# Three edits at the start of a two-block transformer kernel: where the first modulation is summed, how its weights are loaded, and which banks the MLPs' first chunk uses

## What is computed

```python
c_act = silu(c)
for l in range(2):
    mod = c_act @ w_ada[l] + b_ada[l]                   # 1024 x 6144 weights
    shift1, scale1, gate1, shift2, scale2, gate2 = split(mod, 6)
    hdn = rmsnorm(x, norm1_g[l]) * (1 + scale1) + shift1
    proj = hdn @ w_in[l]
    ...                                                 # three attentions, gates, w_out
    x = x + gate1 * (merged @ w_out[l])
    hdn = rmsnorm(x, norm2_g[l]) * (1 + scale2) + shift2
    x = x + gate2 * (square(relu(hdn @ w_ff1[l])) @ w_ff2[l])
```

## Time and profile before

| | |
|---|---|
| median of three runs | 2921.59 us (2919.26 to 2927.62) |
| the profiled execution | 2919.76 us, of which 2917.9 us from the first to the last instruction |
| mean granted TensorE clock | 0.962 |
| PE busy | 2676.1 us, 92% of the span |
| DVE busy | 2125.4 us, 73% |
| ACT busy | 1609.9 us, 55% |
| memory traffic | 666.04 MB, 228 GB/s over the span |
| first matmul of `w_in` (layer 0) | starts at 60.22 us |

### The profile page before, as it was taken

How to read it: one execution, slowest core, us unless ns; L and a number is a source line. 1 busy time by engine, 2 the same in 40 slices (tenths; PEclk the granted TensorE clock), 3 DMA queues, 4 the chain that set the end, 5 groups by cost and what they waited for, 6 DMA issues and landing times.

```text
span 2917.9 us, 39530 instructions
## 1 busy us (share of the span) xinstructions
PE 2676.1 (92%) x12842; PEld 2166.2 (74%) x12842; DVE 2125.4 (73%) x2500; ACT 1609.9 (55%) x2092; POOL 19.9 (1%) x37
## 2 busy tenths in 40 slices
PE   3989989988989999998999888699999999999997
PEld 2767768876767787766898667588878877888885
DVE  6766567776656755855545865689989989989998
ACT  2554444445444444433344544477767777777775
POOL 0000000000000000000000000000000000000000
PEclk9999999998999999999999879799999999999999
DMA  6655458755544565644555420599989999999995
GB/s 233 223 155 166 157 180 264 248 188 166 176 146 152 188 194 165 212 130 141 168 180 173 147 80 30 201 333 344 355 300 363 332 351 331 352 342 334 364 358 206
DMA packets 357967, 666.04 MB, mean 228 GB/s; under 512 B 23008, under 2 KB 57312, under 8 KB 357200
## 3 DMA queue, kind: packets, MB, share of 16 engines
q1 hardware_dynamic: 354080, 648.51, 66.2%
q0 software_dynamic: 3760, 15.91, 1.7%
HBM read 663.29 MB, written 1.05 MB: 228 GB/s over the span
## 4 chain that ended last, share of the span: by engine, by line
PE 80%; DVE 8%; ACT 5%; issue 3%; DVEq 2%; DMA 1%; ACTq 0%; SPq 0%
PE ps L451 44%; PE ps L457 22%; DVE wlo L1884 2%; PE ps L471 2%; PE ps L562 2%; ACT whi L1320 1%; PE ps L476 1%; DVE mod_sum L1908 1%; PE ps L1223 1%; PE ps L661 1%; DMA raw<-in_w_ada 1%; DMA ada_raw<-in_w_ada 1%; PE ps L773 1%; DVEq L1907 0%; PE ps L631 0%
## 5 line engine op out<-in xcount | busy, mean ns | idle before, releaser
L1884 DVE TENSOR_TENSOR wlo<-raw,whi 128x1024 fp32r<-128x1024 f32 x709 | 863.5, 1224 | 469.7 <-ACT whi L1320 459.6
L1320 ACT ACTIVATE whi<-raw 128x1024 fp32r<-128x1024 f32 x709 | 746.8, 1059 | 737.8 <-PE ps L457 630.7
L451 PE MATMUL ps<-whi,xh 128*128 128x512 f32 (+3 forms) x1248 | 457.8, 377 | 12.8 <-issue 9.0
L451 PE MATMUL ps<-whi,xl 128*128 128x512 f32 (+3 forms) x1248 | 445.3, 367 | 0.0
L451 PE MATMUL ps<-whi,gathered_hi 128*128 128x512 f32 x896 | 361.8, 404 | 3.4 <-DVE att L2158 2.6
L451 PE MATMUL ps<-whi,gathered_lo 128*128 128x512 f32 x896 | 355.1, 396 | 0.0
L457 PE MATMUL ps<-wlo,xh 128*128 128x512 f32 (+3 forms) x1248 | 294.6, 363 | 0.0
L457 PE MATMUL ps<-wlo,gathered_hi 128*128 128x512 f32 x896 | 283.4, 397 | 5.4 <-DVE wlo L1884 5.4
L451 PEld LDWEIGHTS ps<-whi,xh 128*128 128x128 f32 x1248 | 241.3, 193 | 56.0 <-issue 14.4
L451 PEld LDWEIGHTS ps<-whi,xl 128*128 128x128 f32 x1248 | 241.5, 193 | 37.3 <-issue 1.9
L457 PEld LDWEIGHTS ps<-wlo,xh 128*128 128x128 f32 x1248 | 217.0, 192 | 38.5
(11 more groups left out here) (390 smaller groups left out, 3577.4 us busy)
## 6 DMA issues: line engine op xcount, KB each, us to landing
raw<-in_moe_w_in SPq DMA_DIRECT2D x227, 512.0 KB, 5.5
spare<-in_moe_w_in SPq DMA_DIRECT2D x165, 512.0 KB, 5.7
mod_b<-in_moe_w_out SPq DMA_DIRECT2D x165, 512.0 KB, 5.4
raw<-in_w_ff SPq DMA_DIRECT2D x128, 512.0 KB, 4.6
raw<-in_w_in SPq DMA_DIRECT2D x96, 512.0 KB, 4.0
work<-in_moe_w_in SPq DMA_DIRECT2D x56, 512.0 KB, 5.6
work<-in_moe_w_out SPq DMA_DIRECT2D x56, 512.0 KB, 5.3
raw<-in_w_ada SPq DMA_DIRECT2D x48, 512.0 KB, 4.8
```

The lines of the kernel that those rows point to most:

```text
L451: e.matmul(ps[0:lhs[2], banks[t], at:at + width], part[:, k0 + j, t * P:t * P + lhs[2]], whi[:, slot, w], start=first and j == 0 and part ...
L1320: e.activation(whi[:, slot, :], src, ACT.Copy).then_inc(split_hi, 1)
L1884: e.tensor_tensor(wlo[:, slot, :], src, whi[:, slot, :].bitcast(F32), ALU.subtract).then_inc(split_lo, 1)
```

## The change

**Loads.** The sixteen loads no longer pass through `raw`. Each has a free buffer and a semaphore of its own (`first_raw`, `first_ready`; in `proj`, `qT`, `kT`, `att` and `mod_a`, unused at that time), and SP issues them without a wait, in the order m = 8, 12, 9, 13, 10, 14, 11, 15, then `x`, then 0, 4, 1, 5, 2, 6, 3, 7. The constants are cut in two: 281 columns (144 KB) first, the rest later by POOL. POOL issues the bias after DVE's first load is summed, the gain after its second, the rest of the constants after its eighth. POOL clears the part of `raw` that the narrow units leave unwritten; SP waits for that once, ahead of the first unit of `w_in`.

**Sums.** DVE now sums only parts 3 (m = 12 to 15) and 1 (m = 4 to 7). Parts 2 and 0 are summed by PE: `c` is spread over 128 columns (`c_rows`, one DVE copy of 128 x 1024), and each 128 x 512 piece of weights is multiplied by it in float32, eight products a part, which leaves the sum in every partition of banks 0 and 2. DVE's work after the sums is cut into halves of 512 columns (`first_scale`, `first_shift`) and runs between its sums; the squares of `x` are taken on ACT as soon as `x` is there. Only one unit of `w_in` is split by DVE ahead of the turned tile 0, where three were. The three bfloat16 tables are made later, in layer 0.

**MLPs.** The first chunk of `mlp` goes to the banks 4 and 5. The next step runs its first half without waiting for the reads of that chunk, and `clear_sums` comes after its second half. In the SwiGLU the odd step now stands ahead of PE's loop.

```diff
-            for _ in range(4):
-                sum_modulation(pe)
+            def first_product(e, m, bank):
+                e.wait_ge(first_ready[m], 16)
+                for j in range(UROWS):
+                    k = m % 4 * UROWS + j
+                    mm = e.matmul(ps[:, bank, :], c_rows[:, k, :], first_raw[m][:, j * 512:(j + 1) * 512], start=k == 0, stop=k == KB - 1)
+                return mm
+            def first_sum(e, half):
+                e.wait_ge(first_used, 4 * half + 4)
+                e.matmul(ps[:, 2 * half + 1, :], k_("ones"), mod_sum[:, half, :], start=True, stop=True).then_inc(mod_summed, 1)
+            for u in range(4):
+                mm = first_product(pe, 8 + u, 0)
+            mm.then_inc(mod_summed, 1)
+            for u in range(4):
+                mm = first_product(pe, u, 2)
+                if u == 0:
+                    first_sum(pe, 0)
+            mm.then_inc(mod_summed, 1)
+            first_sum(pe, 1)
...
-            for m in range(16):
-                add_modulation(dve, m)
-                if m % 4 == 3 and m > 4:
-                    take_modulation(dve)
-            take_modulation(dve)
-            for u in range(LEAD):
-                split(dve, u)
...
+            for u in range(4):
+                first_sums(dve, 12 + u, 0)
+            first_sums(dve, 4, 1)
+            inverse_root(dve, NT)
+            take_gain(dve, 0)
+            dve.wait_ge(bias_ready[2], 16)
+            first_scale(dve, 0)
+            first_sums(dve, 5, 1)
+            first_scale(dve, 1)
+            dve.drain().then_inc(gain_a_used, 1)
+            first_sums(dve, 6, 1)
+            first_sums(dve, 7, 1)
+            for t in range(NT):
+                for n in range(2):
+                    first_shift(dve, t, n)
+                to_pe(dve)
+            split(dve, 0)
             turn_first(dve)
+            for u in range(1, LEAD):
+                split(dve, u)
...
+            def first_scale(e, n):
+                w = slice(D + n * 512, D + (n + 1) * 512)
+                e.wait_ge(mod_summed, n + 1)
+                e.tensor_tensor(mod_b[:, w], ps[:, n, :], mod_b[:, w], ALU.add)
+                e.drain()
+                e.scalar_tensor_tensor(mod_b[:, w], mod_b[:, w], 1.0, gain_a[:, n * 512:(n + 1) * 512], ALU.add, ALU.mult)
+                e.drain()
+                for t in range(NT):
+                    v = work[:, t, n * 512:(n + 1) * 512]
+                    e.scalar_tensor_tensor(v, x[:, t, n * 512:(n + 1) * 512], st[:, 16 + t:17 + t], mod_b[:, w], ALU.mult, ALU.mult)
+                e.drain()
+                for t in range(NT):
+                    v = work[:, t, n * 512:(n + 1) * 512]
+                    e.tensor_tensor(v, v, mod_b[:, n * 512:(n + 1) * 512], ALU.add)
...
-                    group = [(i * UROWS, (0, 1), UCOLS, i == 0, i == 3, UROWS, 0) for i in range(4)]
+                    group = [(i * UROWS, (4, 5), UCOLS, i == 0, i == 3, UROWS, 0) for i in range(4)]
                 by_tile(e, lhs, group, from_turns(src, 1 if kind is SWIGLU else 2))
-                chunks_read(e)
-                clear_sums(e, kind)
                 c.add("chunk")
+                step(e, lhs, hid, kind, first=True)
```

More of the change, by code:

```diff
@@ L65 @@
 SIDE = 24
+FIRST_MODS = 16
+FIRST_LOADS = [m for n in (2, 0) for u in range(4) for m in (4 * n + u, 4 * n + 4 + u)]
 def modulation_schedule():
-    chunks, after, own = [(0, "b", i * 512, i * 512) for i in range(4)], [-1] * 16, [False] * 16
+    chunks, after, own = [(0, "b", i * 512, i * 512) for i in range(4)], [-2] * FIRST_MODS, [True] * FIRST_MODS
     for l in range(DEPTH):
@@ L87 @@
 RAW_MODS = [m for m, own in enumerate(MOD_OWN) if not own]
[L88 removed]
+OWN_MODS = [m for m, own in enumerate(MOD_OWN) if own and m >= FIRST_MODS]
 RAW_OF_MOD = {m: MOD_AFTER[m] + 1 + i for i, m in enumerate(RAW_MODS)}
@@ L352, in program @@
                       + [work[:, i, :] for i in range(NT)] + [spare[:, i, :] for i in range(3)])
+        first_raw = [b.rearrange("p j n -> p (j n)")[:, i * USIZE:(i + 1) * USIZE] for b, n in ((proj[:, :, :], 5), (qT[:, :, :], 2), (kT[:, :, :], 2))
+                     for i in range(n)]
+        first_raw += [b[:, i * USIZE:(i + 1) * USIZE] for b, first, n in ((att, 1, 5), (mod_a, 0, 2)) for i in range(first, first + n)]
+        c_rows = att[:, 0:1024].rearrange("p (k s) -> p k s", k=KB)
         sb_qkv = mod_b[:, :].rearrange("p (t n) -> p t n", t=NT)
@@ L884, in clear_sums, with step @@
                     e.matmul(ps[:, 2 + b, :], zero[0:1, 0:P], zero[0:1, :], start=True, stop=stop)
-            def step(e, lhs, hid, kind, pieces={}, last=False):
-                chunks_read(e)
+            def step(e, lhs, hid, kind, pieces={}, last=False, first=False):
+                if first:
+                    e.wait_ge(evac_act, c.at("chunk", 1))
+                    e.wait_ge(evac_dve, c.at("chunk", 1))
+                else:
+                    chunks_read(e)
                 step_in(e, lhs, kind, 0, pieces)
@@ L923, in body @@
                             step(e, lhs, hid, kind)
-                    loop(e, c, (steps - 1) // pair, body)
-                    for _ in range((steps - 1) % pair):
+                    for _ in range((steps - 2) % pair):
                         step(e, lhs, hid, kind)
+                    loop(e, c, (steps - 2) // pair, body)
                 turn_hidden(e, kind)
@@ L1825, in act_program @@
             act.activation(st[:, 32:128], st[:, 32:128], ACT.Sin).then_inc(act_ready, 1)
-            for u in range(LEAD):
+            act.wait_ge(x_ready, 16)
+            for t in range(NT):
+                act.activation(work[:, t, :], x[:, t, :], ACT.Square, accum_out=st[:, t:t + 1])
+            act.drain()
+            act.activation(st[:, 8:10], st[:, 0:2], ACT.Sqrt, bias=k_("eps"), scale=1.0 / D).then_inc(act_ready, 1)
+            for u in range(LEAD - 1):
                 split(act, u)
-            root_of_squares(act, [x[:, t, :] for t in range(NT)])
             turn(act, xh, KB, by_tile=(0,))
+            split(act, LEAD - 1)
             for l in range(DEPTH):
@@ L2964, in dve_program, with first_sums @@
             dve.drain()
-            for m in range(16):
-                add_modulation(dve, m)
-                if m % 4 == 3 and m > 4:
-                    take_modulation(dve)
-            take_modulation(dve)
-            for u in range(LEAD):
-                split(dve, u)
-            dve.drain()
-            scale_gain(dve, mod_b)
-            dve.wait_ge(x_ready, 16)
-            dve.sem_inc(dve_tick, 1)
-            for _ in range(NT):
-                to_act(dve)
+            def first_sums(e, m, half):
+                total = mod_sum[:, half, :]
+                e.wait_ge(first_ready[m], 16)
+                for j in range(UROWS):
+                    k, w = m % 4 * UROWS + j, first_raw[m][:, j * 512:(j + 1) * 512]
+                    if k == 0:
+                        last = e.tensor_scalar(total, w, c_col[:, k:k + 1], None, ALU.mult)
+                    else:
+                        e.drain()
+                        last = e.scalar_tensor_tensor(total, w, c_col[:, k:k + 1], total, ALU.mult, ALU.add)
+                last.then_inc(first_used, 1)
```

73 lines of the change are left out of this document (49 added, 24 removed).

## The result

| | before | after |
|---|---|---|
| median | 2921.28 us (2919.26 to 2927.62) | 2892.63 us (2892.07 to 2894.55) |
| ratio, 95% interval | | 0.9899 (0.9885 to 0.9912) |
| once more, in the third group below | 2925.5 us | 2890.0 us, 0.9883 (0.9867 to 0.9898) |
| span of the profiled execution | 2917.9 us | 2890.9 us |
| first matmul of `w_in` | 60.22 us | 46.89 us |

A forecast was written before the change was run, and what follows sets the result against it. PE was busy 2676.1 of 2917.9 us, so gains lay where it waits or runs at half clock, most at the start behind DVE's sums. Start 12.2 plus MLPs 11.8 made 24.0 us: 2897.5 from 2921.59, range 2888 to 2909.

The forecast's parts named there:

- Loads: At the start: queues move 370 GB/s, plus 0.9 us for completion, so m = 4 lands at about 26 us.
- PE's products: At the start: PE's float32 products, 0.99 or 2.04 us each, end at 36 us, hidden behind DVE; 43 at worst.
- DVE's chain: At the start: 15.2 us of DVE work behind m = 4, ending at 41.2; tile 0 handed over at 44.2, 13.3 earlier.
- To the first matmul: From tile 0's hand-over to the first `w_in` matmul: 0.8 us lost; the start's net gain is 12.2 us.
- the 0.3 for the bfloat16 tables: In layer 0: three table copies, now made there, cost DVE 0 to 0.6 us, taken as 0.3.
- The MLPs: Behind the first chunks of both ReLU MLPs and in the SwiGLU: waits and low clock go, 4.2 + 4.2 + 3.4 = 11.8 us.
- the rest is the old trace, only earlier: Everything outside the start and MLPs: the old trace unchanged, earlier by 12, then 16, 20 and 24 us.
- rival A: At the start: the last load's landing sets the hand-over, 39.2 us, 5 us better, 2892.5 us in all; chance 0.14.
- B: At the start: SP's queue drops to 300 GB/s, m = 4 lands at 31, 2902.5 us in all; chance 0.10.
- C: In the MLPs: weight slots and loads limit the first steps, the 11.8 us are lost, 2909 us; chance 0.06.
- D: Whole kernel: granted clock falls as PE works more densely; 0.009 eats all, 0.015 gives 2939 us; chance 0.04.
- E: The start gives nothing, since PE waits there for something else: 2910 us; chance 0.02.

The follow-up runs named there:

- third group: The last group of runs, with the kernels before and after measured once more: 2925.5 us before, 2890.0 us after.
- gain_ahead: Changed kernel with scale and gain made by DVE before m = 4's sum, and PE's first sum of ones ahead of m = 0's product: 2887.68 us, ratio 0.9858.
- dve_loads_first: Changed kernel with the last eight loads swapped in pairs, so DVE's chunks land one load earlier and PE's one later: 2891.46 us, ratio 0.9878.
- mlp_only: Kernel before with only the MLPs' part of the change (first chunk in banks 4 and 5, clear behind the next step): ratio 0.9955.
- after_shifted: Changed kernel with 29 idle wait instructions added on DVE ahead of m = 4, moving the expert loop's code: 2899.31 us.
- after_again: The changed kernel, unaltered, run and profiled once more: 2890.0 us.
- pe_kept_busy: Changed kernel with 26 one-row multiplications of zeros on PE ahead of the last sum of ones: hand-over of tile 0 at 43.42 us, unmoved; no whole time given.
- ahead_pe5_filled: Changed kernel with scale and gain before m = 4, m = 5 on PE, and two full float32 filler products behind tile 0's transposes: 2884.11 us, ratio 0.9862.

## Why the prediction was right, and what it missed

**Loads.** Right. m = 4 was summed from 25.23 where I had 26: the queues moved 388 to 413 GB/s from 6 to 22 us, above my 370. No row gives the 0.9 us that I added for the completion of a load; the higher rate hid it in the sum.

The Trainium skill's 358 GB/s (DMA: Bandwidth & Descriptors, Specifications) is exceeded from 6 to 36 us (383 to 413 GB/s), not only in the window of the earlier trace rows.

**PE's products.** Right: hidden, ending at 34.02 (36). They took both prices: 3.78 us for the four records at 23.91, with a granted clock of 0.50 from 24 to 27 us, and 5.56 for twelve from 28.46, at 1.00. The granted clock doesn't tell the price everywhere: the four records at 6.97 took 3.75 us in a window at 1.00, and in the earlier trace rows a sum of ones takes 2.04 us and eight transposes 1.97, although the kernel before has 1.00 from 0 to 60 us. There the times of the instructions are the surer reading.

**DVE's chain.** 15.2 us from 25.23 to 40.44, as added up; `gain_ahead` showed that what leaves it comes through in full. It began 0.8 us earlier than forecast and so ended 0.8 us earlier. The margin to ACT's root was smaller than I had it (0.9 us): the root ended at 26.37, as DVE came to it, and `dve_loads_first` ran into it. The last sum of ones took 2.07 us (2.04) at 0.50; `gain_ahead`, with 1.13 at 1.00, fits the clock as its cause. Hand-over 43.38 (44.2).

**To the first matmul.** From the hand-over to it are 3.51 us where 2.73 were, 0.78 more (0.8). It started at 46.89, in the range of 46 to 50, 13.3 us earlier than before (12.5). The 0.3 for the bfloat16 tables can't be tested: layer 0's attention takes 341.2 to 347.4 us in kernels that all have them there.

**The MLPs.** 4.2 + 4.2 + 2.9 = 11.3 us from the table (SwiGLU: mean of four with the wait 197.6, of ten without it 194.7), where I had 4.2 + 4.2 + 3.4 = 11.8. Wait and clock both count, as `mlp_only` shows; in the SwiGLU the sum is 0.5 too high.

**What was missing: the experts.** The step that failed is the sentence that the rest is the old trace, only earlier. Two stalls of DVE in the experts, 4.1 us each in most profiles (5.85 and 3.72 in the first of before), vanished with the new start, which has 27 instructions fewer on DVE; `after_shifted`, with 29 put back, has both again. With them the sum is 13.3 + 11.3 + 8.2 = 32.8 us. The medians show 28.7 and, in the third group, 35.5; the first profiles 27.0, since before was 4.3 us lucky in its sparse attention and 1.1 in the stretch ahead of it, and the change had the long time in layer 1's attention. With that attention's mean of 3.0 us and 0.4 us lost in the retention layer (221.2 and 221.6 in the means) the sum is 35.4. So 24.0 was 5 to 11 us too small, most of it by a term that no step of the change names. The range held the time because it was wide enough for rival A's 5 us, not because this was foreseen; that part was luck.

**The rivals.** A (landings set the end) fell: DVE had no wait for a load after 25.2 us. B (late loads) fell with 388 to 413 GB/s, although SP could not issue all sixteen at once (last section). C fell with 11.3 us of the MLPs. D fell: the mean clock is 0.959 (0.961 in `after_again`) against 0.962 and 0.958 of before, and no stage became longer by more than chance makes it, but for the 0.4 us of the retention layer. The fall of 0.003 lies in the start: over the first 60 us the column says 1.00 before, with PE busy for 10.2 us at its long prices, and 0.83 after; spread over the span that is 0.0035. E fell at 46.89.

**Open.** Why layer 1's attention takes 340.0 or 342.8 us in two profiles of the changed kernel, and 336.3 to 340.3 in others with its MLPs, was not tried; nor why the sparse attention takes 209.6 or 213.8 us in the kernel before, and 210.8 in two others.

## What to carry to other kernels

Name the things that meet at the start of a chain (here the tenth load and the root of the squares, 0.3 us apart), since the second takes over as soon as the first is moved. Where a saving is larger than the steps explain, compare the trace stage by stage and look also at stages that the edit never touched: the number of instructions ahead of a loop can decide whether its engine stands still at every repetition, here most likely for its code. An engine's idle time marked "issue", with more packets on the instruction queue, is the sign of it, and some idle instructions ahead of the loop are the test.

## What the runs showed of the hardware, unexpected

- DVE stood still for 3.8 to 4.7 us at each repetition of a loop of 304 instructions, with ten more packets on the queue of instructions, and the kernel lost 3.7 to 5.9 us each time, mostly 4.1. Shifting the code by 60 instructions took it away (0.9966, 0.9952 to 0.9979), shifting it by 29 brought it back in another kernel.
- The granted clock fell from 1.00 to 0.50 while PE was busy with multiplications of one row, between 39 and 40 us in `pe_kept_busy`, and stayed at 1.00 under full float32 products in `ahead_pe5_filled`.
- SP can't issue all its loads at once. In the changed kernel eight loads of 0.5 MB are issued by 7.0 us and `x` by 7.6, and then single issues take 3.6 and 5.3 us (timeline of SP's queue); what held them was not tried:

```profile
7.68 3.69 SPq L3243 DMA_DIRECT2D proj<-in_w_ada  x3
11.41 3.59 SPq L3243 DMA_DIRECT2D qT<-in_w_ada  x1
15.05 0.47 SPq L3243 DMA_DIRECT2D proj<-in_w_ada  x1
15.56 5.25 SPq L3243 DMA_DIRECT2D qT<-in_w_ada  x1
```
